# Two attention layers rewritten: heads' steps with projection units between them, one list for the weight ring, outputs turned later

## The chip, the cores and the metric

The kernel runs on one core of a Trainium2 chip. A time is device microseconds (us) of one execution; the number that counts is the median of several executions. Five engines work side by side from queues of their own: TensorE (PE: matrix products and transposes), VectorE (DVE), ScalarE (ACT), GpSimd (POOL) and SyncE (SP, which here issues nearly all transfers). They wait for each other through semaphores, and each runs its own instructions strictly in the written order.

## The reference, cut to what matters

A block of two layers (an "even" and an "odd" one) runs on 256 tokens of width 2048, and after it a second block of two layers (a linear recurrence and a differential attention), which the change does not rewrite. All numbers are float32.

```
def even_layer(x, mem, ...):
    h = rms_norm(x, norm_g) @ w_in                  # 2048 -> 832 + 3072 + 512 + 2560
    c_q, c_kv, k_pe, qkv_b, q_mem, gate = split_cols(h, EVEN_SPLITS)
    q_a = rms_norm(c_q, q_norm_g) @ w_uq            # 8 heads, 128 + 64 (the 64 rotated)
    kv_a = rms_norm(c_kv, kv_norm_g) @ w_ukv
    o_a = causal_attention(q_a, k_a, v_a)           # "MLA", 8 heads
    o_b = moba_attention(q_b, k_b, v_b)             # "MOBA", 8 heads, causal at this length
    o_m = memory_attention(q_mem, mem, ...)         # 4 heads, no mask
    y = jnp.concatenate([o_a, o_b, o_m], -1) * jax.nn.silu(gate)
    return x + y @ w_out                            # 2560 -> 2048
def odd_layer(x, mem, ...):
    h = rms_norm(x, norm_g) @ w_in                  # 2048 -> 6400
    ...    # o_c: "SWA", 16 heads of 64 in a window of 128, 2 key heads, sinks
    ...    # o_d: "DIL", 6 heads, dilated masks;  o_m: memory attention, 4 heads
    y = jnp.concatenate([o_c, o_d, o_m], -1) * jax.nn.silu(gate)
    return x + y @ w_out                            # 2304 -> 2048
# the second block needs silu(c) @ mod_w + mod_b and silu(c_ctx) @ mod_w + mod_b,
# 2048 -> 6144 in both of its layers; nothing before it does
```

## The kernel before, in words

**Products.** A product is made in chunks of 512 output columns. A *unit* is a slice of two blocks of 128 weight rows by 512 columns (512 KB). Float32 accuracy comes from three products of rounded parts: each weight is split in a high part (made by ACT, `hi`, L1004) and a low part (made by DVE, `lo`, L1419), each activation likewise, and `multiply` (L549) issues for each of the 2 token tiles and each of the 2 row blocks three matmuls, 12 in all. So a *projection unit* (P below) needs, in this order: its transfer, ACT's cast, DVE's subtraction, and then PE.

**The ring.** Weights pass through a ring of 4 slots, in three buffers (`ring` for what lands, `ring_hi`, `ring_lo`). Unit U uses slot U mod 4. SP issues the transfers in the order of the units and waits before unit U until `ring` is free of unit U-4: for a projection unit that is when its low part has been made, for a *modulation unit* (M below) when PE has used it. The cast of unit U waits until PE has multiplied unit U-4.

**Modulation units.** The second block's modulation vectors come from 24 chunks of `mod_w` with 8 units each. They need no split: `fill_mod` (L608) multiplies them as they land (8 recorded matmuls for two units). After a chunk DVE copies four partial sums out (`mod_rows`, L1487), PE adds them up (L617) and DVE stores the columns (L1496).

**Attention.** Heads are worked in pairs, a pair is a *turn*: 2 MEM, 4 MOBA, 4 MLA turns in the even layer, 4 + 4 SWA, 3 DIL and 2 MEM turns in the odd one. In `head_loop` one turn is: POOL copies q and k into a staging tile; PE transposes them (L629, L631, for MLA's rotated part L634); ACT copies them out (L1062); PE makes the scores (L645, L648); DVE scales and masks them (L1510) and takes the negated maximum (L1514); ACT takes the exponentials (L1069, L1072); PE transposes these (L657); DVE copies them (L1526); PE multiplies by the values (L673); DVE divides and gates (L1534, L1540) into a tile of its own; PE transposes the gated output (L681), and ACT and DVE split it at once into the parts of the next product (L1079, L1549). In each of the four gaps between PE's steps stand 2 modulation units, 8 in a turn, and no projection.

**The order of stages.** The even layer's input projections (14 chunks of columns, `ev_a` and `ev_b`), 6 turns, the products `uq` and `ukv` for MLA, 4 turns, the output product `ev_out`, transposes of the new x, the odd layer's input projections (`od_b`, `od_c`), 13 turns, and `od_out`. One modulation chunk is made alone within `od_c`. Scores are always 256 by 256 a head, masked or not. The results of a projection chunk leave PSUM (PE's output memory, 8 banks of 512 columns) by ACT (`evict`, L1052, with Silu for the gates); 2 of 4 banks are in use for a chunk.

## Time and profile before

| | |
|---|---|
| median of 3 executions | 2783.96 us (2781.33 to 2784.78) |
| the profiled execution | 2789.43 us |
| its span, first to last instruction | 2787.2 us |
| PE busy | 2591.3 us, 93% |
| DVE busy | 1457.0 us, 52% |
| ACT busy | 1165.8 us, 42% |
| mean granted clock of PE | 0.964 |
| transfers | 424.86 MB, 152 GB/s in the mean |

The busy times are those of the span; what is left outside of the span is 2.2 us. The granted clock is the share of full speed that PE was given: 1.00 is 2.4 GHz, 0.50 is 1.2 GHz, and a value between them is a mean over a stretch that has both. PE is the engine that is nearly always busy, so the questions to ask of the profile are where it idles, where it runs at the lower clock, and what it does in the time that is left.

### The profile page before, as it was taken

What the parts mean: (1) busy time and instruction counts of PE and PEld (TensorE: products, weight loads), DVE (VectorE), ACT (ScalarE), POOL (GpSimd) and SP (SyncE); (2) the same over time, 40 slices, a digit from 0 to 9 for tenths busy, and PEclk for the clock granted to TensorE, in tenths of its full rate; (3) what the DMA queues carried; (4) which work ended last, traced back from release to release, by engine and by line L of the source; (5) the groups of instructions that cost most, each with busy time, mean ns of one, the idle gap of its engine ahead of it and who ended that gap; (6) DMA issues with size and microseconds to landing.
All of it is one profiled execution on the core that took longest, in us unless ns stands there. A gap on an engine that the chain in (4) does not pass through costs nothing.

```text
span 2787.2 us, 33773 instructions
## 1 busy us (share of the span) xinstructions
PE 2591.3 (93%) x12110; PEld 2014.4 (72%) x12110; DVE 1457.0 (52%) x1857; ACT 1165.8 (42%) x1709; POOL 246.1 (9%) x200
## 2 busy tenths in 40 slices
PE   6999998889899997889799999999799999999988
PEld 5888885548788864448577777778677787777766
DVE  4644544444544534355546676743436565463764
ACT  5445442323444422134545555622433334243442
POOL 0000001000000000000144555300000000000000
PEclk9999999999999998699899999999999999999999
DMA  5566667675566667696323333233244334242423
GB/s 205 186 193 189 194 193 258 212 250 183 152 193 195 190 194 255 214 307 233 116 82 91 98 94 90 79 114 98 61 121 121 99 91 120 83 128 83 121 91 121
DMA packets 275085, 424.86 MB, mean 152 GB/s; under 512 B 14374, under 2 KB 92988, under 8 KB 273852
## 3 DMA queue, kind: packets, MB, share of 16 engines
q1 hardware_dynamic: 273596, 418.28, 49.1%
q10 hardware_dynamic: 1408, 5.51, 0.5%
q8 instruction: 49, 0.80, 0.1%
q14 instruction: 32, 0.26, 0.0%
HBM read 421.65 MB, written 2.10 MB: 152 GB/s over the span
## 4 chain that ended last, share of the span: by engine, by line
PE 85%; DVE 7%; ACT 4%; issue 2%; DMA 1%; SPq 0%; DVEq 0%; ACTq 0%
PE ps L549 59%; PE ps L793 13%; PE ps L608 3%; PE ps L800 2%; PE ps L673 2%; PE ps L645 1%; PE ps L617 1%; ACT ring_hi L1004 1%; DVE head_stats L1514 1%; ACT arena L1069 1%; DVE ring_lo L1419 1%; PE ps L885 1%; DVE arena L1510 1%; PE ps L903 1%; PE ps L590 1%
## 5 line engine op out<-in xcount | busy, mean ns | idle before, releaser
L1004 ACT CAST ring_hi<-ring 128x1024 fp32r<-128x1024 f32 (+2 forms) x590 | 614.7, 1044 | 1126.0 <-PE ps L549 968.0
L1419 DVE TENSOR_TENSOR ring_lo<-ring,ring_hi 128x1024 fp32r<-128x1024 f32 (+2 forms) x526 | 634.9, 1211 | 847.8 <-ACT ring_hi L1004 845.6
L549 PE MATMUL ps<-ring_hi,act_hi 128*128 128x512 f32 (+2 forms) x1272 | 496.1, 390 | 18.7 <-DVE act_lo L1458 7.6
L549 PE MATMUL ps<-ring_hi,features_hi 128*128 128x512 f32 x1152 | 463.1, 402 | 37.0 <-DVE features_lo L1771 15.3
L549 PE MATMUL ps<-ring_lo,act_hi 128*128 128x512 f32 (+2 forms) x1272 | 494.1, 388 | 0.0
L549 PE MATMUL ps<-ring_hi,act_lo 128*128 128x512 f32 (+2 forms) x1272 | 493.7, 388 | 0.0
L549 PE MATMUL ps<-ring_lo,features_hi 128*128 128x512 f32 x1152 | 453.9, 394 | 0.0
L549 PE MATMUL ps<-ring_hi,features_lo 128*128 128x512 f32 x1152 | 453.5, 394 | 0.0
L549 PEld LDWEIGHTS ps<-ring_hi,features_hi 128*128 128x128 f32 x1152 | 219.1, 190 | 106.7 <-issue 41.9
L549 PEld LDWEIGHTS ps<-ring_hi,act_hi 128*128 128x128 f32 x1272 | 242.5, 191 | 71.1 <-issue 11.6
L549 PEld LDWEIGHTS ps<-ring_lo,act_hi 128*128 128x128 f32 x1272 | 242.6, 191 | 48.4
L549 PEld LDWEIGHTS ps<-ring_hi,act_lo 128*128 128x128 f32 x1272 | 242.1, 190 | 48.2
L549 PEld LDWEIGHTS ps<-ring_hi,features_lo 128*128 128x128 f32 x1152 | 219.3, 190 | 47.3
L549 PEld LDWEIGHTS ps<-ring_lo,features_hi 128*128 128x128 f32 x1152 | 219.5, 191 | 42.9
L793 PE MATMUL ps<-features_hi,ring_hi 128*128 128x512 f32 x512 | 206.6, 403 | 3.8 <-DVEq L1777 3.8
L793 PE MATMUL ps<-features_lo,ring_hi 128*128 128x512 f32 x512 | 200.2, 391 | 0.0
L793 PE MATMUL ps<-features_hi,ring_lo 128*128 128x512 f32 x512 | 200.2, 391 | 0.0
L2049 POOL TENSOR_TENSOR ring_lo<-ring,ring_hi 128x1024 fp32r<-128x1024 f32 x64 | 168.9, 2647 | 274.9 <-ACT ring_hi L1004 274.7
L608 PE MATMUL ps<-ring,cond_t 128*32 128x512 f32 x768 | 124.6, 673 | 2.8 <-DMA ring<-in_mod_w 2.7
L2036 POOL COPY arena<-proj 128x256 f32 (+1 forms) x38 | 17.2, 452 | 1191.6 <-PE ps L631 439.8
L793 PEld LDWEIGHTS ps<-features_hi,ring_hi 128*128 128x128 f32 x512 | 96.8, 189 | 27.3 <-issue 7.6
L793 PEld LDWEIGHTS ps<-features_lo,ring_hi 128*128 128x128 f32 x512 | 96.9, 189 | 23.2 <-issue 3.6
(226 smaller groups left out, 2507.8 us busy)
## 6 DMA issues: line engine op xcount, KB each, us to landing
ring<-in_mod_w SPq DMA_DIRECT2D x192, 512.0 KB, 4.5
ring<-in_att_w_in SPq DMA_DIRECT2D x128, 512.0 KB, 3.8
ring<-in_ev_w_in SPq DMA_DIRECT2D x104, 512.0 KB, 4.3
ring<-in_od_w_in SPq DMA_DIRECT2D x96, 512.0 KB, 3.7
ring<-in_lru_w_in SPq DMA_DIRECT2D x64, 512.0 KB, 4.2
ring<-in_ev_w_out SPq DMA_DIRECT2D x40, 512.0 KB, 3.7
ring<-in_od_w_out SPq DMA_DIRECT2D x36, 512.0 KB, 4.4
ring<-in_lru_w_out SPq DMA_DIRECT2D x32, 512.0 KB, 3.7
```

The lines of the kernel that those rows point to most:

```text
L549: mm = pe.matmul(PS[:, bank, 0:n], a, w[:, k - k0, :], start=(k == 0 and j == 0), stop=(k == kt - 1 and j == 2))
L590: mm = pe.transpose(PS[:, 4 + q % 4, col:col + P], rows(tt, 2 * j + k), ident)
L608: mm = pe.matmul(PS[g:g + 32, bank, :], CS[:, 2 * k:2 * k + 32], RA[:, U % SLOTS, k % 2 * CHUNK:(k % 2 + 1) * CHUNK], start=(k < 4), stop= ...
L617: mm = pe.matmul(PS[:, bank, 2 * j:2 * j + 2], rows[:, j * P:(j + 1) * P], SEL[:], start=True, stop=True)
L645: mm = pe.matmul(PS[:, 6 + a, tt * SEQ:(tt + 1) * SEQ], qk[:, tt * P:(tt + 1) * P], qk[:, SEQ:2 * SEQ], start=True, stop=not mla)
L673: mm = pe.matmul(PS[:, 6 + a, tt * P:tt * P + w], PT[:, a, kt * SEQ + tt * P:kt * SEQ + (tt + 1) * P], v, start=(kt == 0), stop=(kt == TT ...
L793: mm = pe.matmul(PS[:, part * 2 + b, :], W[:, U % SLOTS, w], x[:, kk, :], start=(kk == 0 and j == 0), stop=(kk == KT - 1 and j == 2))
L800: mm = pe.matmul(PS[:, 4 + j, :], GW[:, b, j, :], XC[:, b, :, :].rearrange("p c s -> p (c s)"), start=True, stop=True)
L885: mm = pe.matmul(PS[:, 4 + c, :], DQK[64 * c:64 * c + 64, j, CHUNK + tt * P:CHUNK + (tt + 1) * P], DQK[64 * c:64 * c + 64, j, 0:CHUNK], st ...
L1004: act.copy(WH[:, U % SLOTS, 0:n], RA[:, U % SLOTS, 0:n]).then_inc(s_hi, 1)
L1419: dve.tensor_tensor(out=WL[:, U % SLOTS, 0:n], in0=RA[:, U % SLOTS, 0:n], in1=WH[:, U % SLOTS, 0:n].bitcast(F32), op=ALU.subtract).then_in ...
L2049: pool.tensor_tensor(out=WL[:, U % SLOTS, :], in0=RA[:, U % SLOTS, :], in1=WH[:, U % SLOTS, :].bitcast(F32), op=ALU.subtract).then_inc(s_l ...
```

## The change

Both layers are written anew around one list, `RING`, of all units in their order. The list is laid out at build time. A turn (`Turn`) now has four gaps that hold *projection units of later chunks* and modulation units together. With P for a projection unit, M for a modulation unit and a bar for each step of PE in the turn (scores, transposes of the weights of attention, values), the gaps are, as the list has them:

| turns | gaps |
|---|---|
| MEM 0, 1, MOBA 0 (even) | PPP, PPMMPPMMP, PPMMPP, PPMMP |
| MOBA 1, 3 | PPP, PPMMPPMMP, PPMMP, PPMMP |
| MOBA 2 | PPP, PPMMPMMP, PPMMP, PPMMP |
| MLA 0, 1 | MM, PMMP, MM, MM |
| MLA 2, 3 | MM, PMM, MM, MM |
| SWA, 8 turns, and DIL 0 | P, PMMPMMP, PMMP, PMM (DIL 0: third gap PMM) |
| DIL 1, 2 | P, PMMPMM, PMM, PMM |
| MEM 0, 1 (odd) | P, PMMMM, PMM, PMM; P, PMMPMM, PMM, MM |

Only the chunks that the first turns need (two of `ev_b`, three of `od_b`) are made before the turns. MLA's P are the first units of `ev_out`. The modulation chunk that stood alone is mixed into the last `od_b` chunk before the turns. Further:

- ACT and DVE follow the list: `follow` makes, for each unit of a gap, the split of the unit 4 (ACT) or 3 (DVE) places on, and evicts a chunk after its last unit.
- Three PSUM banks instead of four serve the projections of the turns, each half of a chunk is awaited and released by itself, and `multiply` now does all row blocks of one token tile before the next tile.
- Masks that leave a block empty are used: scores are 384 columns a head instead of 512, 3 blocks instead of 4 are transposed and multiplied.
- q and k are transposed straight from their rows; POOL's staging is gone. SWA's two key heads are doubled and transposed once.
- The gated output overwrites the gate; the transposes of y and their splits come later, two blocks at a time: between the `ukv` units, between the first units of `ev_out`, and beside the first 9 units of `od_out`.
- The transposes of the new x stand between the last units of `ev_out`.
- The copies of two inputs of the second block (ctx, final gain) are issued some units later in `od_out`.

```diff
-            def head_loop(h):
-                ...
-                    fill_mod(mod, 0, i)
...
+EV_PRE, OD_PRE = (6, 11), (0, 2)
+EV_FILL, OD_FILL = (0, 2, 4, 9, 1, 3, 5, 10, 7, 8), (1, 9, 3, 4, 5, 6, 10, 11, 7)
+SPREAD = ((), (0, 1), (2,), (3,))
+MLA_TURNS = lay_turns(6, [(MLA, 0, (0, 2, 0, 0)), (MLA, 1, (0, 2, 0, 0)), (MLA, 2, (0, 1, 0, 0)), (MLA, 3, (0, 1, 0, 0))],
+                      [("ev_out", u) for u in range(4, 10)], ((0,), (1,), (2,), (3,)))
...
+                for m, bank in tiles:
+                    if hold is not None and m in hold:
+                        pe.wait_ge(*hold[m])
+                    for k in range(k0, k0 + nk):
                         xh, xl = x(k, m)
...
+            def head_turn(turn):                       # PE
...
+                if h is MLA:
+                    pe.wait_ge(s_ge, evicted("ukv", i))
+                    pe.wait_ge(s_ys, n0)
+                for a in range(1 if h.pair else 2):
+                    ...                                # transposes of q and k
+                fill(turn.gaps[0])
+                if turn.mod:
+                    sum_mod(turn.mod - 1, 2 if h is MLA else MB)
+                ...                                    # scores
+                fill(turn.gaps[1])
+                ...                                    # transposes of the exponentials
+                fill(turn.gaps[2])
+                if h.mem is None:
+                    pe.wait_ge(s_ge, evicted(*value_chunk(turn)))
+                ...                                    # values
+                fill(turn.gaps[3])
...
+            def follow(units):                         # ACT
+                for unit in units:
+                    U = POS[unit]
+                    hi_to(U + SLOTS)
+                    if U in LAST_OF:
+                        evict(*LAST_OF[U])
+                    hi_to(U + SLOTS + 1)
...
+            def follow(units):                         # DVE
+                for unit in units:
+                    lo_to(POS[unit] + SLOTS)
+                    ropes_behind(*unit)
...
+            def head_turn(turn):                       # DVE
+                follow(turn.gaps[0])
+                if turn.mod:
+                    mod_columns(turn.mod - 1, 2 if h is MLA else 3)
+                ...                                    # mask, maximum
+                follow(turn.gaps[1])
+                ...                                    # copies of the transposed exponentials
+                follow(turn.gaps[2])
+                dve.wait_ge(s_ge, evicted(*gate_chunk(turn)))
+                ...                                    # division and gate
+                follow(turn.gaps[3])
+                mod_rows(turn.mod)
```

**SP's queue in a SWA turn.** Before, in the turns of the odd layer, SP issued modulation units alone. `weight_units_used` counts the units that PE has multiplied; the rows around the transfer are the loop's own.

```order
L438 DMA ring<-in_mod_w 128x2x512 [waits weight_units_used] x8
L452 UNCONDITIONAL_BRANCH
L452 ISA
L438 ISA [waits weight_units_used]
L438 DMA ring<-in_mod_w 128x2x512
L436 REGISTER_ALU
```

Now a SWA turn is this; `weights_lo_by_vector` counts the low parts made by DVE, and the name behind "waits" is what frees the slot, so it tells what stood in the slot four places earlier.

```order
L581 DMA ring<-in_od_w_in 128x2x512 [waits weights_lo_by_vector]
L581 DMA ring<-in_mod_w 128x2x512 [waits weights_lo_by_vector]
L581 DMA ring<-in_mod_w 128x2x512 [waits weight_units_used]
L581 DMA ring<-in_od_w_in 128x2x512 [waits weight_units_used]
L581 DMA ring<-in_od_w_in 128x2x512 [waits weights_lo_by_vector]
L581 DMA ring<-in_mod_w 128x2x512 [waits weight_units_used] x2
L581 DMA ring<-in_od_w_in 128x2x512 [waits weights_lo_by_vector] x2
L581 DMA ring<-in_mod_w 128x2x512 [waits weight_units_used] x2
L581 DMA ring<-in_od_w_in 128x2x512 [waits weights_lo_by_vector] x2
L581 DMA ring<-in_mod_w 128x2x512 [waits weight_units_used] x2
```

What moved: projection transfers (`in_od_w_in`) now stand between the modulation transfers, and the fourth row is a projection unit whose slot a modulation unit held.

**DVE in an MLA turn.** Before, in the MLA loop: division and gate of the turn's second head (L1534, L1540), the copy of the modulation chunk's sums (L1487), the low parts of the output (L1549), and no unit of the ring. ISA rows only set up the instruction below them.

```order
L1534 RECIPROCAL head_stats<-head_stats 128x2 [waits head_out]
L1540 ISA [waits head_recip]
L1540 SCALAR_TENSOR_TENSOR arena<-ps,head_stats,proj 128x128
L1540 ISA
L1540 SCALAR_TENSOR_TENSOR arena<-ps,head_stats,proj 128x128
L1486 ISA
L1487 COPY proj<-ps 128x512 [waits weight_units_used]
L1549 ISA [waits head_y_hi]
L1549 TENSOR_TENSOR act_lo<-ps,act_hi 128x256
L1549 ISA [waits head_y_hi]
L1549 TENSOR_TENSOR act_lo<-ps,act_hi 128x256
```

Now, at the end of the first MLA turn, from the same division to the first mask of the next turn:

```order
L1816 RECIPROCAL head_stats<-head_stats 128x2 [waits head_out]
L1822 SCALAR_TENSOR_TENSOR proj<-ps,head_stats,proj 128x128 [waits head_recip]
L1822 SCALAR_TENSOR_TENSOR proj<-ps,head_stats,proj 128x128
L1639 TENSOR_TENSOR ring_lo<-ring,ring_hi 128x1024 [waits weights_hi]
L1725 COPY proj<-ps 128x512 [waits weight_units_used]
L1733 TENSOR_TENSOR mod_t<-ps,vectors_t 128x8 [waits mod_summed]
L1786 SCALAR_TENSOR_TENSOR arena<-ps,consts_first 128x384 [waits head_scores]
```

What moved: the low part of a projection unit of the next turn (L1639) stands ahead of the copy of the modulation sums (L1725), on which the next turn's first modulation unit waits; the output's low part (L1549) is gone from here.

## Rows read from the trace of the kernel before

**Rows 1.** The page, first section: busy us, share of the span, instructions.

```profile
PE 2591.3 (93%) x12110; PEld 2014.4 (72%) x12110; DVE 1457.0 (52%) x1857; ACT 1165.8 (42%) x1709; POOL 246.1 (9%) x200
```

**Rows 2.** PE's waits: waiter <- releaser: us in total, times, longest us.

```profile
PE ps L657 <- ACT head_stats L1072: 22.9, 16, 2.2
...
PE ps L657 <- ACT arena L1069: 19.6, 26, 1.0
...
PE ps L681 <- DVE arena L1540: 12.1, 3, 4.1
```

**Rows 3.** Busy time by stage: stretch, length, busy per engine, clock, DMA, GB/s.

```profile
168.10:429.40 261.30, 261.30 (x1161) 216.25 (x1159) 119.62 (x113) 121.54 (x136) 1.43 (x4) 1.00 0.66 190
429.40:519.10 89.70, 73.46 (x505) 43.62 (x504) 49.40 (x106) 30.09 (x79) 7.70 (x20) 0.97 0.87 288
519.10:549.00 29.90, 29.84 (x120) 24.11 (x120) 12.51 (x15) 13.61 (x18) 1.65 (x4) 0.92 0.48 156
549.00:624.20 75.20, 63.83 (x384) 34.65 (x384) 32.17 (x68) 23.14 (x62) 4.95 (x12) 0.97 0.70 233
624.20:736.00 111.80, 111.77 (x482) 92.26 (x483) 52.45 (x46) 41.17 (x39) 0.00 (x0) 0.97 0.62 191
736.00:748.40 12.40, 4.09 (x32) 3.17 (x30) 10.66 (x19) 10.95 (x20) 0.00 (x0) 0.76 0.30 86
748.40:1014.70 266.30, 266.29 (x1180) 220.69 (x1184) 121.17 (x113) 117.44 (x125) 3.81 (x3) 0.99 0.61 181
1014.70:1037.00 22.30, 17.71 (x109) 10.77 (x108) 4.15 (x7) 3.94 (x7) 0.00 (x0) 0.92 0.75 245
1037.00:1256.70 219.70, 178.23 (x1052) 97.63 (x1051) 99.95 (x253) 54.16 (x163) 13.60 (x43) 0.82 0.77 257
1256.70:1357.10 100.40, 100.37 (x432) 82.58 (x432) 46.55 (x47) 46.17 (x53) 6.32 (x3) 0.98 0.68 219
sum 1189.00, PE 1106.89 PEld 825.72 DVE 548.62 ACT 462.20 POOL 39.46; mean PE 110.69 PEld 82.57 DVE 54.86 ACT 46.22 POOL 3.95
```

**Rows 4.** L549 alone in a stretch of projections: length, busy, clock.

```profile
211.60:429.40 217.80, 217.80 (x960) 1.00 0.65 188
```

**Rows 5.** A MOBA turn by time: start, length, engine, line [idle before].

```profile
459.05 1.06 PE L608 MATMUL ps<-ring,cond_t 128*32 128x512 f32 x8
...
460.04 1.99 PE L645 MATMUL ps<-arena 128*128 128x256 f32 x8
...
463.81 0.66 PE L657 MATMUL ps<-consts,arena 128*128 128x128 f32 x4 [0.61 <-ACT arena L1069]
...
466.70 2.05 PE L673 MATMUL ps<-proj,arena 128*128 x16
...
469.93 0.69 DVE L1487 COPY proj<-ps 128x512 f32<-128x512 f32 x1 [0.22 <-PE ps L608]
```

**Rows 6.** The last MOBA turn by time: uq units behind modulation units.

```profile
506.49 1.10 PE L608 MATMUL ps<-ring,cond_t 128*32 128x512 f32 x8
...
507.58 10.02 SPq L438 DMA_DIRECT2D ring<-in_ev_w_uq  x6
...
511.73 1.05 ACT L1004 CAST ring_hi<-ring 128x1024 fp32r<-128x1024 f32 x1 [5.88 <-DMA ring<-in_ev_w_uq]
...
513.38 1.05 ACT L1004 CAST ring_hi<-ring 128x1024 fp32r<-128x1024 f32 x1 [0.59 <-DMA ring<-in_ev_w_uq]
...
512.81 1.23 DVE L1419 TENSOR_TENSOR ring_lo<-ring,ring_hi 128x1024 fp32r<-128x1024 f32 x1 [5.52 <-ACT ring_hi L1004]
```

**Rows 7.** ACT by time in the second block, changing its table.

```profile
2154.07 1.28 ACT L1315 ACT_TABLE_LOAD   x1
2155.37 1.08 ACT L1315 ACTIVATE second_block<-ps 128x512 f32<-128x512 f32 x2
```

**Rows 8.** Stretches with PE idle first, columns as in rows 3.

```profile
2153.80:2157.20 3.40, 0.69 (x5) 0.54 (x4) 1.89 (x2) 3.35 (x5) 0.00 (x0) 1.00 0.54 154
2642.40:2650.60 8.20, 4.34 (x14) 3.42 (x13) 4.70 (x10) 6.50 (x13) 0.00 (x0) 0.79 0.23 77
```

More of the change, by code:

```diff
@@ new lines, with __init__, with_mod @@
+class Turn:
+    def __init__(self, number, heads, i, mod, gaps):
+        self.number, self.heads, self.i, self.mod, self.gaps = number, heads, i, mod, gaps
+        self.even = heads in (MEM_EV, MOBA, MLA)
+def with_mod(units, m, pairs):
+    out, n = [], len(units)
+    after = {}
+    for j, p in enumerate(pairs):
+        after.setdefault(-(-(j + 1) * n // (len(pairs) + 1)), []).append(p)
+    for k in range(n + 1):
+        for p in after.get(k, []):
+            out += [("mod", 8 * m + 2 * p), ("mod", 8 * m + 2 * p + 1)]
+        out += units[k:k + 1]
+    return out
@@ new lines, in lay_turns, with chunk_units @@
+def lay_turns(first, plan, units, mod_gaps):
+    turns, at = [], 0
+    for j, (heads, i, counts) in enumerate(plan):
+        number = first + j
+        m = number if number < MOD_ALONE else number + 1
+        gaps = []
+        for count, pairs in zip(counts, mod_gaps):
+            gaps.append(with_mod(units[at:at + count], m, pairs))
+            at += count
+        turns.append(Turn(number, heads, i, m, gaps))
+    assert at == len(units)
+    return turns
+def chunk_units(stage, chunks, per=8):
+    return [(stage, per * c + j) for c in chunks for j in range(per)]
@@ new lines, with _queue @@
+OD_TURNS = lay_turns(10, [(SWA[j], i, (1, 3, 2, 1)) for j in range(2) for i in range(4)]
+                     + [(DIL, 0, (1, 3, 1, 1)), (DIL, 1, (1, 2, 1, 1)), (DIL, 2, (1, 2, 1, 1)), (MEM_OD, 0, (1, 1, 1, 1)), (MEM_OD, 1, (1, 2, 1, 0))],
+                     chunk_units("od_b", OD_FILL) + chunk_units("od_c", [0]), SPREAD)
+OUT_C1_AHEAD = [("ev_out", 10 + u) for u in range(4, 10)]
+OD_LAST_PRE = with_mod(chunk_units("od_b", [8]), MOD_ALONE, range(4))
+RING = []
+def _queue(units):
+    RING.extend(units)
@@ new lines, with units_of, multiplied, unit_width @@
+CHUNK_UNITS = {"uq": 2, "ukv": 1, "ev_out": 10, "od_out": 9}
+def units_of(stage):
+    return CHUNK_UNITS.get(stage, 8)
+def multiplied(stage, c):
+    return max(POS[stage, u] for u in range(c * units_of(stage), (c + 1) * units_of(stage))) + 1
+def unit_width(stage, u):
+    if stage == "ev_a" and u >= 8:
+        return 2 * (EV_LAT - EV_CKV)
+    return 2 * (OD_IN % CHUNK) if stage == "od_c" else UNIT
+EVICTED = ([(stage, c) for stage in ("mkv0", "mkv1", "ev_a") for c in range(2)] + [("ev_b", c) for c in EV_PRE + EV_FILL]
+           + [("uq", c) for c in range(3)] + [("ukv", c) for c in range(4)] + [("od_b", c) for c in OD_PRE + (8,) + OD_FILL] + [("od_c", 0)])
@@ new lines, in rows_free, with gate_chunk, value_chunk @@
+def rows_free(bank, before):
+    return max(2 * e + w + 1 for e in range(EVICTED.index(before)) for w in range(2) if BANKS[EVICTED[e]][w] == bank)
+def gate_chunk(turn):
+    h, i = turn.heads, turn.i
+    if h is MEM_OD:
+        return ("od_b", 11) if i == 0 else ("od_c", 0)
+    if h is DIL:
+        return "od_b", 10 + i // 2
+    if h in SWA:
+        return "od_b", 8 + SWA.index(h)
+    return "ev_b", {"mem_ev": 11, "moba": 9 + i // 2, "mla": 7 + i // 2}[h.name]
+def value_chunk(turn):
+    h, i = turn.heads, turn.i
+    if h.mem is not None:
+        return None
+    if h is MLA:
+        return "ukv", i
+    return ("ev_b", 4 + i // 2) if h is MOBA else ("od_b", 6 if h is DIL else 2)
@@ new lines, in _ @@
+            pe.wait_ge(s_ge, evicted("od_c", 0))
+            for p in range(3):
+                y_transposes_of("od", p)
+            for p in range(9):
+                pe.wait_ge(s_ye, YT_AT["od", p] + 1)
+                od_out(p)
+                for q in (range(3, 5), range(5, 7), range(7, 9))[p] if p < 3 else ():
+                    if q >= 7:
+                        pe.wait_ge(s_ys, 2 * (q + 15))
+                    y_transposes_of("od", q)
+                if p == 2:
+                    sum_mod(N_MOD - 1)
@@ L771, in _ @@
+            for u in range(9, 36):
+                od_out(u)
             pe.wait_ge(s_re, RES0["lru_out"])
```

1117 lines of the change are left out of this document (600 added, 517 removed).

## The prediction

> **What bounds the kernel now.** First the page: PE is busy for 2591.3 us, 93% of the span [rows 1]; no other engine passes 52%. So a change pays where PE idles or runs slowly, or where it takes work from PE. Second the waits of PE: in the turns PE waits before the transposes of the exponentials (L657) for ACT, 22.9 and 19.6 us in all, and before the transposes of y (L681) for DVE, 12.1 us in three waits of about 4 us, one at the end of each run of turns [rows 2]. Third the stretches, cut by stage, from the first `ev_b` unit at 168.1 us to the last `od_out` unit at 1357.1 us [rows 3]. They are 1189.0 us long and PE is busy for 1106.9, so 82.1 us are idle: 16.2 in the first six turns (89.70 less 73.46), 11.4 in the MLA turns, 41.5 in the 13 odd ones, 8.3 at the transposes of x. The projections between them have none. The same rows hold a second loss, the clock: 1.00 in the projections, 0.82 in the odd turns. Busy time times the missing share is, in the order of the rows, 0, 2.2, 2.4, 1.9, 3.4, 1.0, 2.7, 1.4, 32.1 and 2.0, together 49 us. So PE has 1106.9 - 49 = 1058 us of work at full clock in 1189 us.
>
> **What the change takes from PE.** Matmuls of projections and modulation stay as many as they were. In the 19 masked turns half of the score records shrink to half (8 records in 1.92 us, from 460.04 to the next step: -0.5), 2 of 8 transposes go (4 take 0.66: -0.3) and 4 of 16 value records (2.05 us: -0.5) [rows 5]; that is 1.3 a turn, 25 us. MLA's rotated part and SWA's doubled keys add some 4. So 29 us, and 1029 us of work are left. If PE never waited, the stretch would end 1189 - 1029 = 160 us earlier. POOL's copies go too, but PE waited little for them; the matmul order within a unit costs nothing (the same 12 matmuls), in the second block it moves a wait by a few matmuls, which I put at 0, with 2 us to either side.
>
> **The filling.** A projection unit (P) takes 12 records of 217.8/960 us, 2.72 us [rows 4]; two modulation units (M) take 0.99 us, from 459.05 to 460.04, so 0.5 each [rows 5]. The chain from scores to exponentials is about 5 us; a gap of PPMMPPMMP lasts 15.6 us and even PMMPMMP 10.2 us. So the waits of L657 go, all 42.5 us, and the clock has dense work.
>
> **What is late next: the ring.** An M leaves its slot only when PE has used it, and the unit four places on may then be a P, which needs transfer, cast and subtraction. The trace shows this once, where `uq` follows the last turn. PE ends a pair of M begun at 506.49; the transfers are issued from 507.58; the casts are at 511.73 and 513.38, 1.05 us each; the first subtraction runs from 512.81 for 1.23 us [rows 6]. So a P in the slot of the pair's first M is ready at 514.04, 6.5 us after PE left the pair, and one in the slot of the second at 513.38 + 1.05 + 1.23 = 515.66, 8.1 us after. In PMMPMMP the last P stands in the slot of the second M (the row of SP's queue that waits for `weight_units_used` ahead of `in_od_w_in`). Between them PE has one P and two M, 3.7 us: it waits 4.4. The bounds are 2.8 (ready as a first one) and 4.4; I take 3.9, nearer to the row that shows it. Such places: 8 SWA turns, DIL 0, MOBA 2, and the chunk ahead of the odd turns, 11 of them, 43 us. In PPMMPPMMP two P and more stand between, 6.6 us or more against 6.5: nothing. Elsewhere:
> - DIL 1, 2: two such P each with 4.4 and 5.7 us of cover, 5 us a turn, 10 us. Odd MEM turns: PMMMM covers only 3.4 us of the exponentials' chain, and `od_c` units are half as long; 8 us a turn, 16 us. First `od_out` unit: silu eviction, division, then transposes, ACT and DVE for the first pair of y: 5 us.
> - MLA: the low part of the next turn's P stands on DVE ahead of the copy of the modulation sums, and PE's first M of the next turn waits for that copy. The P is in the slot of the last pair's first M, so the copy ends 6.5 + 0.7 us later [rows 5, 6]; PE has 0.5 (M) + 1 (waiting for the division) + 1.3 (transposes), so it waits 4.4 at three turn starts, 13. Waits of 1.5 inside each turn and 3.5 at the exit to `ev_out` make it 23 us (10 to 30).
> - Start of the first turn, MOBA's small waits, the way into MLA: 10 us.
> - ACT changes tables between Silu and Exp. Eight silu chunks now leave within turns. A change is 1.28 us, and the activation follows at once [rows 7]. The next chunk's second tile needs the bank after 1.36 us of matmuls; table and first half (1.28 + 0.54) end at 1.8, so 0.5 each, 4 us.
>
> What the Trainium skill says of the last point, in ScalarE: Activation LUTs, section "What ACT_TABLE_LOAD costs", is more: about 1.28 us of load and as much again of drain at each change, 2.66 us, with the advice to group by table set, which this change goes against. The trace shows the load and no drain behind it. By the page's figure the term would be some 15 us instead of 4.
>
> - The clock: after an idle time of 2.7 us PE stays at 1.00, after one of 3.9 us the next stretch shows 0.79, a piece at 1.2 GHz [rows 8]. Some 15 new waits lie between; 1 us each, 15 us.
>
> **The sum.** 43 + 10 + 16 + 5 + 23 + 10 + 4 + 15 = 126 us of new waits against 160: the change wins 34 us. The profiled execution would be 2789.4 - 34 = 2755 us (span 2753); the median of the runs shown lies 5.5 us lower, 2784.0 - 34 = 2750 us. Tell apart from no change can a measurement 0.2%, 5.6 us. With every wait at its low bound (11 x 2.8, MLA 10, the others halved, the clock 0) it is some 65 us, a gain of 95; with the high ones (48, 30, 45, 10, and 25 for the clock) 160, a gain of nothing.
>
> **Rivals.**
> *The cover holds* (2688 us). Transfers may be issued earlier than I place them and land in 3.5 us, DVE and ACT may be ahead, and the clock never falls. For it: in the projections DVE is busy for 46% and ACT for 47% (119.62 and 121.54 of 261.3) [rows 3], so nothing but latency stands against it. Against it: [rows 6]. Waits of 65 us: 2784 - 95.
> *The clock falls with each wait* (2809 us, slower). A wait of 4 us once a turn, then a stretch at 1.2 GHz, in which P takes 5.4 us. For it: the odd turns had waits of at most 2.2 us and yet 0.82 [rows 2, 3]. Against: they were full of short, narrow steps, and now two thirds of a turn are dense matmuls. Price: these turns now hold 72 P, 11 us of `od_c` and 13 times 10 us of M and steps, 337 us; at 0.82 they take 411, 74 more. 160 - 111 (126 without the clock term) - 74 = -25. It decides from 0.9 downwards.
>
> The Trainium skill speaks for this one, in TensorE: Matmul & The Clock Gate, section "HAM oscillation — how this bites in real kernels": where a wait for a transfer comes back in every tile, the clock is lost anew each time. The trace agrees in kind (0.79 after 3.9 us), not in 2.7 us.
>
> *The transfers are the bound* (2784 us, no change). 478 units pass the ring in the stretch. Two back to back landed 1.65 us apart by their casts (511.73 and 513.38) [rows 6]: 789 us, less than 1029. Only the turns with few P come near. Little speaks for it.
>
> **Chances.** Forecast 0.50, cover holds 0.25, clock 0.15, transfers or anything else that gives the gain back 0.10. The time is the forecast's, 2750 us, its own range 2722 to 2778. The range for 8 in 10 goes from 2692, short of the second case, to 2792, short of the third. Faster by more than 0.2%: all of the first two and half of the last, 0.80; the other half is no change, 0.05; slower 0.15.
>
> **What would show it.** Right: waits of L657 for ACT gone; per SWA turn one wait of PE's projections of 3 to 4 us for DVE's low part, beside a shorter one for a modulation transfer, and nothing of the kind in MEM and MOBA turns except MOBA 2; at three MLA turn starts PE waiting for the copy of the sums; the stretch up to the end of `od_out` 20 to 50 us shorter, and from there to the end the same length. The filling is wrong if L657 still waits for ACT. The sum is wrong if the clock of the odd stage stays under 0.9, or if the SWA turns have no wait at all.

## The result, and the profile after

The changed kernel takes 2827.51 us (median of 4, 2824.62 to 2831.30), the one before, beside it, 2784.37. The ratio is 1.0151, 95% interval 1.0126 to 1.0177: 42 us slower, where 34 us faster was forecast. The profiled execution took 2831.3 us, its span is 2829.2.

First the page of the changed kernel, its first section (busy us, share of the span, instructions). PE is busy for 9 us more than in [rows 1], although it has 126 matmuls fewer.

```profile
PE 2600.0 (92%) x11984; PEld 2005.9 (71%) x11984; DVE 1435.1 (51%) x1900; ACT 1158.1 (41%) x1698; POOL 215.4 (8%) x120
```

Next the waits of PE in the changed kernel (us in total, times, longest), to be read against [rows 2].

```profile
PE ps L674 <- DVE ring_lo L1639: 77.0, 43, 4.6
PE ps L743 <- DVE proj L1725: 19.2, 3, 7.0
...
PE ps L674 <- DVE act_lo L1772: 7.3, 1, 7.3
PE ps L743 <- DMA ring<-in_mod_w: 6.0, 10, 1.3
```

The waits for the exponentials, 42.5 us, are gone. In their place stand waits for low parts of projection units (77.0 us), the copy of the modulation sums at three MLA turn starts (19.2), the low part of y ahead of `od_out` (7.3), and modulation transfers (6.0).

Then the stretch from the first `ev_b` unit to the last `od_out` unit, cut by stage, columns as in [rows 3]: `ev_b` ahead of the turns, even turns with their projections, `ukv`, MLA turns, `ev_out`, `od_b` ahead of the turns, the chunk with the lone modulation chunk, odd turns with their projections, `od_out`, and last what follows it.

```profile
168.10:213.90 45.80, 44.50 (x202) 36.35 (x201) 24.26 (x34) 25.75 (x39) 0.00 (x0) 1.00 0.64 195
213.90:554.35 340.45, 313.92 (x1487) 235.65 (x1487) 142.11 (x192) 130.59 (x179) 0.00 (x0) 0.96 0.62 205
554.35:568.90 14.55, 14.15 (x66) 11.64 (x66) 10.30 (x18) 9.51 (x16) 0.00 (x0) 0.88 0.38 115
568.90:687.80 118.90, 93.14 (x416) 53.97 (x416) 28.72 (x66) 23.23 (x58) 0.00 (x0) 0.76 0.50 167
687.80:779.70 91.90, 91.88 (x420) 76.12 (x421) 52.55 (x61) 39.30 (x48) 0.00 (x0) 0.98 0.58 187
779.70:837.90 58.20, 58.20 (x263) 48.04 (x261) 28.84 (x32) 29.55 (x35) 0.00 (x0) 1.00 0.59 176
837.90:867.00 29.10, 23.61 (x109) 15.37 (x109) 11.37 (x23) 8.72 (x9) 2.27 (x6) 0.94 0.74 253
867.00:1289.00 422.00, 371.05 (x1889) 252.34 (x1887) 171.17 (x340) 135.24 (x247) 0.00 (x0) 0.94 0.66 220
1289.00:1401.80 112.80, 105.52 (x478) 87.39 (x476) 57.65 (x67) 54.59 (x66) 6.14 (x3) 0.95 0.66 218
1401.80:2829.20 1427.40, 1339.93 (x5985) 1066.71 (x5984) 816.96 (x926) 612.86 (x881) 206.75 (x108) 0.97 0.33 98
```

The last row is what lies behind the rewritten layers: 1427.4 us, as before (2787.2 - 1357.1 = 1430.1). So all of the loss in the profiled execution is in the stretch, which is now 1233.7 us long instead of 1189.0. Length less busy time, row by row, is 117.7 us of idle time. Busy time times the missing share of the clock is 0, 12.6, 1.7, 22.4, 1.8, 0, 1.4, 22.3 and 5.3, together 67.5. The account of the stretch, beside what was forecast:

| us | before | forecast | after |
|---|---|---|---|
| work at full clock | 1058 | 1029 | 1048 |
| PE idle | 82 | 111 | 118 |
| lost to the clock | 49 | 15 | 68 |
| the stretch | 1189 | 1155 | 1234 |

The work at full clock is what is left of a length without the other two; with granted clocks of two digits it is good to a few us. The idle time was forecast within 7 us. The clock is off by 53, the work by 19.

Where the clock goes is seen in one SWA turn. First PE, ACT, DVE and SP by time (start, us, engine, line, [idle before]), without the rows of weight loads and the projection matmuls ahead; then three stretches around the wait.

```profile
950.38 1.14 PE L743 MATMUL ps<-ring,cond_t 128*32 128x512 f32 x8
...
951.48 0.88 SPq L581 DMA_DIRECT2D ring<-in_mod_w  x2
951.75 1.04 ACT L1222 CAST ring_hi<-ring 128x1024 fp32r<-128x1024 f32 x1 [2.43 <-DMA ring<-in_od_w_in]
952.83 2.52 DVE L1639 TENSOR_TENSOR ring_lo<-ring,ring_hi 128x1024 fp32r<-128x1024 f32 x2 [6.06 <-ACT ring_hi L1222]
...
954.11 0.50 PE L674 MATMUL ps<-ring_hi,act_hi 128*128 128x512 f32 x1 [2.59 <-DVE ring_lo L1639]
```

```profile
926.00:951.00 25.00, 23.65 (x130) 15.77 (x128) 11.06 (x25) 9.07 (x18) 0.00 (x0) 1.00 0.63 212
954.10:957.50 3.40, 3.39 (x9) 2.72 (x10) 1.23 (x1) 0.00 (x0) 0.00 (x0) 0.58 1.02 372
957.60:971.00 13.40, 13.40 (x74) 9.47 (x72) 4.89 (x12) 3.14 (x3) 0.00 (x0) 0.98 0.55 194
```

PE waits 2.59 us for the low part of the last unit of the gap PMMPMMP, the place where a wait was forecast. Then it works for 3.4 us at a granted clock of 0.58, mostly at 1.2 GHz, and at 0.98 after that. The wait of 2.6 us costs 1.4 us more (3.39 x 0.42).

The start of the second MLA turn shows the order on two engines at once (weight loads, transfers and ACT's other copies are left out):

```profile
589.35 0.38 PE L804 MATMUL ps<-consts,proj 128*64 128x128 f32 x2
...
593.79 1.04 ACT L1222 CAST ring_hi<-ring 128x1024 fp32r<-128x1024 f32 x1 [12.39 <-DMA ring<-in_ev_w_out]
594.74 0.58 ACT L1317 COPY arena<-ps 128x512 f32<-128x512 f32 x1
594.87 1.22 DVE L1639 TENSOR_TENSOR ring_lo<-ring,ring_hi 128x1024 fp32r<-128x1024 f32 x1 [6.78 <-ACT ring_hi L1222]
...
596.01 0.68 DVE L1725 COPY proj<-ps 128x512 f32<-128x512 f32 x1
...
596.75 1.94 PE L743 MATMUL ps<-ring,cond_t 128*32 128x512 f32 x8 [7.01 <-DVE proj L1725]
...
598.61 1.87 PE L754 MATMUL ps<-row_sums,proj 128*128 128x2 f32 x8
```

The copy of the sums (L1725) stands behind the low part (L1639), that behind ACT's cast (L1222), and that waits for a transfer. ACT's copies of q and k (L1317) stand behind the same cast. PE idles for 7.01 us, and its next steps run at half speed: the granted clock from 596.7 to 600.3 is 0.50, and eight small matmuls (L754) take 1.87 us, where 1.05 us is their time at full clock (at 448.07 in the run `plain` below).

### The profile page after: what moved, and what is told of

Same layout as the page of the kernel before. It is cut to its first block, busy times and chain, and to the rows that moved or that the text cites. A ratio compares the mean times of both kernels' runs of the same rounds, so it can differ in the third digit from the quotient of the medians.

```text
span 2829.2 us, 31394 instructions
## 1 busy us (share of the span) xinstructions
PE 2600.0 (92%) x11984; PEld 2005.9 (71%) x11984; DVE 1435.1 (51%) x1900; ACT 1158.1 (41%) x1698; POOL 215.4 (8%) x120
## 4 chain that ended last, share of the span: by engine, by line
PE 79%; DMA 9%; DVE 6%; ACT 5%; issue 1%; SPq 1%; ACTq 0%; DVEq 0%
PE ps L674 55%; PE ps L1011 12%; DMA ring<-in_od_w_in 5%; DVE ring_lo L1639 2%; ACT ring_hi L1222 2%; DMA ring<-in_ev_w_in 2%; PE ps L743 2%; PE ps L1018 2%; PE ps L822 1%; PE ps L1103 1%; DMA ring<-in_ev_w_out 1%; PE ps L754 1%; PE ps L1121 1%; PE ps L719 1%; PE ps L844 1%
## 5 line engine op out<-in xcount | busy, mean ns | idle before, releaser
L1222 ACT CAST ring_hi<-ring 128x1024 fp32r<-128x1024 f32 (+2 forms) x590 | 611.6, 1038 | 1337.4 <-PE ps L674 776.8
L1639 DVE TENSOR_TENSOR ring_lo<-ring,ring_hi 128x1024 fp32r<-128x1024 f32 (+2 forms) x526 | 634.2, 1209 | 898.2 <-ACT ring_hi L1222 893.4
L674 PE MATMUL ps<-ring_hi,act_hi 128*128 128x512 f32 (+2 forms) x1272 | 528.8, 416 | 92.6 <-DVE ring_lo L1639 73.7
L674 PE MATMUL ps<-ring_lo,act_hi 128*128 128x512 f32 (+2 forms) x1272 | 508.1, 399 | 0.0
L674 PE MATMUL ps<-ring_hi,act_lo 128*128 128x512 f32 (+2 forms) x1272 | 507.5, 399 | 0.0
L674 PEld LDWEIGHTS ps<-ring_hi,act_hi 128*128 128x128 f32 x1272 | 250.0, 197 | 203.6 <-DVE ring_lo L1639 113.2
L674 PEld LDWEIGHTS ps<-ring_hi,act_lo 128*128 128x128 f32 x1272 | 250.1, 197 | 54.1
L674 PEld LDWEIGHTS ps<-ring_lo,act_hi 128*128 128x128 f32 x1272 | 251.1, 197 | 46.1
L743 PE MATMUL ps<-ring,cond_t 128*32 128x512 f32 x768 | 123.9, 624 | 25.3 <-DVE proj L1725 19.2
L1011 PEld LDWEIGHTS ps<-features_hi,ring_lo 128*128 128x128 f32 x512 | 96.7, 189 | 20.3
```

Of the source, the lines that this page charges most:

```text
L674: mm = pe.matmul(PS[:, bank, 0:n], a, w[:, k - k0, :], start=(k == k_first and j == 0), stop=(k == k_last and j == 2))
L743: mm = pe.matmul(PS[g:g + 32, MB, :], CS[:, 2 * k:2 * k + 32], RA[:, U % SLOTS, k % 2 * CHUNK:(k % 2 + 1) * CHUNK], start=(k < 4), stop=(k ...
L1011: mm = pe.matmul(PS[:, part * 2 + b, :], W[:, U % SLOTS, w], x[:, kk, :], start=(kk == 0 and j == 0), stop=(kk == KT - 1 and j == 2))
L1222: act.copy(WH[:, U % SLOTS, 0:n], RA[:, U % SLOTS, 0:n]).then_inc(s_hi, 1)
L1639: dve.tensor_tensor(out=WL[:, U % SLOTS, 0:n], in0=RA[:, U % SLOTS, 0:n], in1=WH[:, U % SLOTS, 0:n].bitcast(F32), op=ALU.subtract).then_in ...
```

## The experiments

Times are given as the ratio to the kernel before, timed on the same chip. The changed kernel has 1.0151; 0.01 is 28 us. The runs stand on three chips, so what is won or lost is told by the ratios and not by the medians.

**Matmuls in the waits (`warm`).** `dense(n, bank)` issues n matmuls of 512 columns (384 where a first column is given) of `act_hi` by itself into a bank that is free there.

```diff
+                    if wait and at == len(units) - 1 and stage != "mod" and units[at - 1][0] == "mod":
+                        dense(wait, 4)          # wait = 10, second gap, not MLA
...
+                if h is MLA and i:
+                    dense(34, 2, P)             # ahead of the first gap; 20 more at MLA's exit
```

> The changed kernel, with matmuls that nobody reads put where PE waits: ten of 512 columns (2.3 us) ahead of the last projection unit of the second gap in the 15 turns where that unit follows modulation units (it waited 2.5 to 3.0 us), 34 of 384 columns (5.8 us) at the starts of MLA turns 1 to 3 (5.7 to 7.0 us waited), 20 of them at MLA's exit (4.6 us). Nothing is made earlier, so the waits only turn into work. Theory 'the clock': these waits cost the granted clock as well, some 55 us at the lower level behind the waits of the even and odd turns and 60 us in the MLA turns. Then the clock of the MLA turns goes from 0.76 to 0.95 or more, of the odd turns from 0.94 to 0.97, and the time falls by 40 to 55 us, to 2772 to 2787. Rival 'idle time only' (the clock falls for the narrow modulation matmuls or the short attention steps, waits or not): clock and time unchanged, or up to 10 us longer.

Measured: 1.0015 (0.9993 to 1.0036), so 38 us won, though the added matmuls make nothing that is used. Even, MLA and odd turns in this run:

```profile
214.10:542.50 328.40, 318.55 (x1552) 239.57 (x1553) 144.46 (x194) 132.27 (x180) 0.00 (x0) 1.00 0.64 215
554.50:681.30 126.80, 120.06 (x582) 81.76 (x583) 36.43 (x77) 27.43 (x62) 0.00 (x0) 0.85 0.52 175
846.50:1258.00 411.50, 381.10 (x1982) 258.55 (x1980) 172.96 (x341) 137.78 (x249) 0.00 (x0) 0.98 0.67 229
```

The clock is 1.00 instead of 0.96, 0.85 instead of 0.76, and 0.98 instead of 0.94. In MLA it rises less than the 0.95 that were expected; what is left there was not looked for. That idle time costs the clock is shown.

**Narrow matmuls in the waits (`warm_narrow`).**

```diff
-                    pe.matmul(PS[:, bank, first:CHUNK], ATH[:, 0:P], ATH[:, first:CHUNK], start=True, stop=True)
+                    pe.matmul(PS[0:32, bank, first:CHUNK], ATH[:, 0:32], ATH[:, first:CHUNK], start=True, stop=True)
```

> The run with dense matmuls in the waits, but the added matmuls use 32 columns of the array instead of 128 (as the modulation matmuls do), as many and as long ones, at the same places. Theory 'any work keeps the clock': as with the dense ones, 2791, clock of the MLA turns as there. Rival 'the columns of the array count': narrow matmuls keep the clock no better than idling, the stretches at the lower clock come back, 2815 to 2827.

Measured: 0.9988 (0.9966 to 1.0010), at least as fast as with the wide ones. The even, MLA and odd turns show 1.00, 0.90 and 0.98. Matmuls of 32 columns keep the clock no worse than those of 128, so that the modulation units are narrow is not what lowers it. It is the idle time.

**The order on DVE (`rows_first`), and on ACT as well (`rows_act`).**

```diff
+                if h is MLA:                    # DVE
+                    mod_rows(turn.mod)
                 follow(turn.gaps[3])
...
+                if h is MLA and turn.i:         # ACT, behind the copies of q and k; rows_act only
+                    follow(MLA_TURNS[turn.i - 1].gaps[3])
```

> The changed kernel, with the copy of the modulation sums ahead of the low parts on DVE at the end of the four MLA turns. PE's wait for that copy (19.2 us in three) goes. Theory 'two engines': ACT has the same order (the cast of the next projection unit stands ahead of the copies of q and k), so PE waits before the scores instead, and of 7.0 us only some 4.4 are won at each start: 13 us of waiting, and with the clock 15 to 20 us, 2807 to 2812. Rival 'DVE alone': all 19 us and the clock behind them, 35 us, 2792. Rival 'the unit itself': the projection unit behind the scores is late by what was won, nothing is won.

> As the run before this one, and on ACT the cast of the next turn's projection unit stands behind the copies of q and k. Theory 'two engines': now the whole wait goes at the three starts, 19 us, and most of the 57 us at the lower clock in the MLA turns, 20 us more: 2827 - 39 = 2788. Rival 'the unit itself' (its transfer lands 8 us after the slot is free, its cast and low part follow): a wait of 2 to 4 us before the first projection unit takes the place, and the win is 20 us or less, 2807 or above.

Measured: 1.0088 (1.0057 to 1.0119) and 1.0009 (0.9983 to 1.0034): 18 and 40 us won. The MLA turns with the first `ev_out` units, 130.0 us long and at 0.76 in the changed kernel, in the two runs:

```profile
560.60:674.00 113.40, 99.29 (x460) 59.39 (x461) 36.56 (x77) 27.33 (x62) 0.00 (x0) 0.85 0.59 199
```

```profile
562.90:664.20 101.30, 90.91 (x460) 54.84 (x461) 36.52 (x77) 27.70 (x62) 0.00 (x0) 0.93 0.68 223
```

In `rows_first` PE's wait for the copy of the sums (19.2 us) is gone, and in its place stand 3.6 us before the scores for ACT's copies (L822 for L1319), as the theory 'two engines' has it in kind; it had put some 8 us there. In `rows_act` these are gone too. The wait is the queues' order, not the unit's transfer. With DVE's order mended ACT's still holds PE; ACT's alone was not tried. The stretch tells 29 of the 40 us, the rest is not placed.

**Half of each modulation transfer (`half_mod`).** SP moves 256 of the 512 columns, so the modulation vectors are made from other numbers.

```diff
-                    unit(U, t["mod_w_2"][layer], 2 * j, 2, chunk * CHUNK, CHUNK)
+                    unit(U, t["mod_w_2"][layer], 2 * j, 2, chunk * CHUNK, CHUNK, part=2)
```

> The changed kernel, but a modulation unit moves only the first half of its columns (256 KB instead of 512 KB); PE multiplies as before, with what stands in the other half of the slot. The modulation sums are so computed from other numbers. Theory 'burst': behind a modulation pair SP issues up to four transfers at once, they land 1.3 us apart, and the projection unit among the last is late by the two modulation transfers ahead of it. With those at half, it lands 1.3 us earlier: PE's wait for low parts falls from 77 us to about 45, with the clock 35 to 45 us are won, 2785 to 2792. Rival 'latency': the 4 us from issue to landing and the 2.3 us of cast and subtraction are all there is, the waits stay within 10 us of 77 and the time within 10 us of 2827.

Measured: 1.0021 (0.9998 to 1.0043), 36 us won, but not as expected:

```profile
PE ps L674 <- DVE ring_lo L1639: 71.1, 42, 4.8
```

The waits for low parts fell by 6 us, not by 32. The odd turns became 20 us shorter (402.2 instead of 422.4), of which idle time is 6 (402.20 - 357.12 = 45.1 against 50.9); 9 are busy time of the modulation matmuls (58.8 instead of 67.6 us for 416 records; the last section tells why a late transfer lengthens them), the rest other busy time, which holds the clock. The time fits the theory, its place does not. That the transfers' bytes count is shown. That they count as a burst ahead of the projection unit is not: the wait it was to shorten stayed.

**The order of units in the SWA turns (`regroup`, `alt`).** The units of each of the 8 turns are laid out anew, where they were P|PMMPMMP|PMMP|PMM.

```diff
+for _turn in OD_TURNS[:8]:
+    singles(_turn, "P|PMMPPMM|PMM|PPMM")          # regroup
+    singles(_turn, "P|MPMPMPM|PMPM|PMM")          # alt
```

> The changed kernel with the units of the 8 SWA turns in the order P|PMMPPMM|PMM|PPMM: modulation units in pairs as before, two projection units between the pairs where they can be. Theory 'the slot': waits of 2.6 us a turn instead of 3.9, in two pieces of about 1 to 1.5 us, behind which the clock stays: 10 us of waiting and 8 us of clock: 2827 - 18 = 2809. Rival 'rate': 2827.

> The changed kernel with the units of the 8 SWA turns in the order P|MPMPMPM|PMPM|PMM instead of P|PMMPMMP|PMMP|PMM (the same units in the same gaps, but modulation units single). Theory 'the slot' (a projection unit is late where it follows a modulation unit into its slot with less than 6.5 us of PE's work between): of four such places a turn two are left with more cover, the waits of a turn fall from 3.9 us to 2.4 and none is over 1 us, so the clock stays: 12 us of waiting and 10 us of clock in the eight turns, less 5 us for 24 more changes between the two kinds of matmul: 2827 - 17 = 2810. Rival 'rate' (the transfers of a turn take as long in any order): the waits stay 31 us in eight turns and the changes of kind are added: 2832.

Measured: 1.0078 (1.0044 to 1.0113), 20 us won, and 1.0214 (1.0185 to 1.0243), 18 us lost. Regrouped, the odd turns are 405.7 us long instead of 422.4. With single units PE's waits are as the slot theory has them, 42.7 us for low parts down to 17.4 in the odd turns, but two new costs stand beside them. The groups of that run in the odd turns:

```profile
L685 PE MATMUL ps<-ring_hi,act_hi 128*128 128x512 f32 (+1 forms) x320 | 135.7, 424 | 17.7 <-DVE ring_lo L1650 17.4
...
L754 PE MATMUL ps<-ring,cond_t 128*32 128x512 f32 x416 | 91.8, 632 | 1.8 <-DMA ring<-in_mod_w 1.6
...
L765 PE MATMUL ps<-row_sums,arena 128*128 128x2 f32 x104 | 15.5, 271 | 21.1 <-DVE arena L1736 21.1
```

The same groups of the changed kernel:

```profile
L674 PE MATMUL ps<-ring_hi,act_hi 128*128 128x512 f32 (+1 forms) x320 | 139.3, 435 | 43.2 <-DVE ring_lo L1639 42.7 <-ACT proj L1295 0.3
...
L743 PE MATMUL ps<-ring,cond_t 128*32 128x512 f32 x416 | 67.6, 613 | 2.6 <-DMA ring<-in_mod_w 2.5
...
L754 PE MATMUL ps<-row_sums,arena 128*128 128x2 f32 x104 | 12.6, 243 | 3.6 <-DVE arena L1725 3.6
```

The same 416 modulation matmuls take 24 us more, while those of the projections take 388 instead of 398 us. And PE waits 21.1 instead of 3.6 us for the copy of the sums, which now stands behind a late low part on DVE, as in MLA.

**The last odd turn (`od_exit`).** On DVE the division, the copy of the sums and the first y stand ahead of `od_out`'s low parts. On ACT the first y stands ahead of their casts.

```diff
+                if last:                        # DVE, ahead of follow(turn.gaps[2])
+                    mod_rows(turn.mod)
+                    y_lo_of("od", 0)
...
+                    y_hi_of("od", 0)            # ACT, behind the last eviction
```

> The changed kernel, but in the last odd turn DVE does the division ahead of the low parts of od_out's first units, and ACT and DVE split the first pair of y ahead of the casts and low parts behind it. PE waited 7.3 us for that low part (1290.6 to 1297.8) and ran 10 us at the lower clock behind it. Theory 'queue order': od_out's first unit is then ready by its own transfer (landed 1290.6 plus 2.3 us), 4.8 us earlier, and with the clock 5 to 8 us are won: 2820. Rival 'the transfer': the next units are late by the same, nothing is won, 2827.

Measured: 1.0147 (1.0118 to 1.0176), no difference to 1.0151 that can be told. The stage itself, from the last turn's end, became 5.7 us shorter, 108.6 instead of 114.3 with a clock of 0.98 instead of 0.96:

```profile
1291.40:1400.00 108.60, 104.92 (x478) 86.86 (x476) 58.02 (x63) 55.77 (x67) 7.29 (x4) 0.98 0.68 230
```

Only the profile speaks for the queue's order here.

**No mixing (`plain`).** The projections stand ahead of the turns (`uq` and MLA's `ev_out` units behind them), the modulation pairs in the turns as before; the rest of the change stays, but for the PSUM bank of the modulation sums.

```diff
-SPREAD = ((), (0, 1), (2,), (3,))
+SPREAD = ((0,), (1,), (2,), (3,))
...
+            fill(EV_AHEAD)
             for turn in EV_TURNS:
...
+            fill(OD_AHEAD)
             for turn in OD_TURNS:
```

> The change without its mixing: all projections of a layer ahead of its turns (uq between the even turns and ukv, ev_out behind MLA), two modulation units in each of a turn's four gaps as in the kernel before; the halved masked blocks, the missing staging, the late transposes of y and the order within a unit stay as in the changed kernel. Theory 'mixing costs': the projections run at their 2.72 us again, the even turns with their projections take 314 us instead of 342, MLA with its 91 instead of 119, the odd ones 402 instead of 422, although the waits for the exponentials and the clock of 0.82 in the odd turns come back: 2827 - 76 = 2752. Rival 'the waits for the exponentials cost as much': within 10 us of 2827. Rival 'something else in the change costs' (its copies, the late transposes): 2800 or above.

Measured: 0.9830 (0.9805 to 0.9855), median 2747.15 us: by the ratios 89 us faster than the changed kernel and 47 faster than the one before. The profiled execution took 2757.5, 10 us above the median. The even turns with seven `uq` units behind them, the MLA turns with the first `ev_out` units, and all projections and turns of the odd layer behind its third chunk:

```profile
433.00:536.30 103.30, 90.58 (x533) 52.83 (x534) 46.34 (x101) 33.91 (x77) 0.00 (x0) 0.98 0.85 287
547.20:644.90 97.70, 92.05 (x461) 54.31 (x460) 37.49 (x77) 27.98 (x62) 0.00 (x0) 0.91 0.67 232
815.80:1214.70 398.90, 365.76 (x1891) 248.42 (x1889) 173.83 (x338) 127.34 (x239) 0.00 (x0) 0.95 0.73 231
```

The odd part is 23.5 us shorter than mixed, the MLA part 32.3, although PE again waits for exponentials, 33.0 us in all. The longer part of these, and all its waits for low parts in the whole kernel:

```profile
PE ps L833 <- ACT head_stats L1335: 17.4, 16, 1.8
PE ps L678 <- DVE ring_lo L1650: 17.3, 8, 3.7
```

**Matmuls in the waits for exponentials: in the kernel before (`before_dense`), and without mixing (`plain_dense`).** The edit of the first is shown; the second has the same in its SWA turns and three such matmuls in each other turn but MLA's.

```diff
+                        for _ in range((8, 4)[a] if pair else 0):
+                            pe.matmul(PS[:, 2, :], ATH[:, 18 * SEQ:18 * SEQ + P], ATH[:, 18 * SEQ:20 * SEQ], start=True, stop=True)
                         pe.wait_ge(s_ex, n(a, 1))
```

> The kernel before, with matmuls that nobody reads ahead of the waits for the exponentials in the 8 SWA turns: 8 of 512 columns (1.8 us) ahead of the first head's transposes (2.0 to 2.2 us waited), 4 (0.9 us) ahead of the second's (1.2 us waited). Theory 'the clock falls with PE's density': the odd turns run at 0.82 because their steps are short, so dense work in the gaps lifts the clock there to 0.9 or more; 10 to 15 us of the 32 us lost are won: 2770 to 2775. Rival 'the kind of matmul' (modulation matmuls of 32 columns and the narrow steps count as little, whatever stands between): clock 0.82 to 0.84, time as before or up to 5 us longer.

> The same, with matmuls that nobody reads in the waits for the exponentials: 8 and 4 of 512 columns in a SWA turn, 3 in the other turns but MLA's. By what such matmuls won in the kernel before (22 us): 2730. If the turns without staging have shorter waits, so that the added matmuls outlast them: as without them, 2752, or up to 10 us more.

Measured: 0.9921 (0.9894 to 0.9949) and 0.9842 (0.9810 to 0.9873). In the kernel before, 22 us are won, more than expected; its odd turns are 193.2 us long, not 219.7 as in [rows 3], at a clock of 0.98 instead of 0.82:

```profile
1036.00:1229.20 193.20, 173.21 (x1141) 99.84 (x1141) 99.41 (x252) 54.03 (x163) 13.52 (x43) 0.98 0.86 289
```

Without mixing nothing is won in the median, where 22 us were expected: the clock of the odd part rises from 0.95 to 1.00, but PE's busy time from 365.8 to 377.9 us.

```profile
810.70:1203.60 392.90, 377.90 (x2003) 262.88 (x2001) 175.02 (x340) 128.34 (x240) 0.00 (x0) 1.00 0.74 236
```

**What won, together (`best`).** `rows_act`, `regroup` and `od_exit`, with 9 matmuls in the wait of the second gap and 18 at MLA's exit.

```diff
-                fill(turn.gaps[1])
+                fill(turn.gaps[1], 0 if h is MLA else 9)
```

> The changed kernel with what won put together: the two orders on DVE and ACT in the MLA turns (39 us by their run), the SWA turns regrouped (18 us), the last odd turn's order (0 to 6 us), and nine dense matmuls in the wait of the second gap of the even turns and the first DIL turn (10 us or more by the stretch of the even turns in the run with dense matmuls). If the parts add up, 2827 - 39 - 18 - 3 - 12 = 2755; if each only moves a wait that another one hides, 2785 or above.

Measured: 0.9844 (0.9810 to 0.9879), median 2752.94 us on a chip where the kernel before takes 2793.97. By the ratios 86 us are won over the changed kernel, where 72 were expected; the two intervals leave some 12 us to either side. So no part is hidden by another. With `plain` at 0.9830 (0.9805 to 0.9855) the two cannot be told apart: mending the order, with matmuls in what waits are left, wins as much as taking the mixing out.

## Why the prediction was wrong

**Right.** The bound is PE, and the change acts in the stretch alone. The waits of L657 went. The ring's wait came where it was placed: 2.6 us per SWA turn for the low part, with shorter ones for modulation transfers; I took 3.9 us a turn, and 2.8 as the lowest. MLA came out at 25.8 us of idle time (118.90 - 93.14) against 23: three starts of 7.0, 6.5 and 5.7 instead of 4.4, an exit of 4.6, less within the turns. `rows_act` confirms the mechanism, which the forecast had seen on DVE but not on ACT. Idle time in all was 118 us against 111. PE's waits for evictions are 8.6 and 1.6 us in the whole kernel against 3.1 before, where I put 4 for the table changes; but in the longest one (3.15 us, at 499.4) no table is loaded, ACT's eviction stands behind a cast that waited for its transfer.

**Right in the sum only.** For PPMMPPMMP I forecast no wait, since two projection units cover it. It waits 2.5 to 3.0 us in each of five turns, as here in the second even turn:

```profile
291.89 1.40 SPq L581 DMA_DIRECT2D ring<-in_mod_w  x2
293.34 5.59 SPq L581 DMA_DIRECT2D ring<-in_ev_w_in  x3
...
300.30 1.04 ACT L1222 CAST ring_hi<-ring 128x1024 fp32r<-128x1024 f32 x1 [8.30 <-DMA ring<-in_ev_w_in]
...
302.66 0.78 PE L674 MATMUL ps<-ring_hi,act_hi 128*128 128x512 f32 x1 [2.56 <-DVE ring_lo L1639]
```

I counted from the slot's release to one transfer's landing. The unit was issued at 293.34, right behind a pair of modulation units, and its cast began 7 us later. These 13 us made good what the SWA turns did not cost (8 x 1.3 = 10 us), so that the idle time comes out within 7 us is in part luck.

**Wrong: the clock's term, 15 us, measured 68.** The step that failed is "after an idle time of 2.7 us PE stays at 1.00, after one of 3.9 us the next stretch shows 0.79 [rows 8]; some 15 new waits lie between; 1 us each". I took a bound between two cases from a part of the kernel in which PE had worked densely, and I let the 49 us that the old stretch lost vanish with it. After 2.6 us PE did fall, in seven of the eight SWA turns: the lower level is granted within 1 us of the wait's end or before it. The number of waits was off as well: 26 in the stretch are 2 us or longer, and 68 us over 26 waits are 2.6 us each, not 1. In MLA, waits of 6 to 7 us were followed by steps at half speed, 22 us by the row. `warm`, with 38 us won by matmuls that only fill the waits, shows that this is the waits' doing for most of the 53 us. The rival "the clock falls with each wait" was the right one in kind and sign. It was priced at 0.82 for all of a turn, and came out at 0.94 to 0.96 in the large stages and 0.76 in MLA. Its sum of 2809 us lies on the right side and 18 us short, and it had a chance of 0.15.

The sentence that the Trainium skill put beside that rival (TensorE: Matmul & The Clock Gate, section "HAM oscillation — how this bites in real kernels": a wait that recurs in every tile loses the clock anew) agrees with the trace and with `warm`: the clock fell anew in seven of eight SWA turns.

**Wrong: the work, 1029 us, measured 1048.** Between projections a modulation pair costs more than the 1.0 us at which it was taken:

```profile
961.74 0.39 PE L674 MATMUL ps<-ring_hi,act_lo 128*128 128x512 f32 x1
962.06 1.07 PE L743 MATMUL ps<-ring,cond_t 128*32 128x512 f32 x8
963.06 0.50 PE L674 MATMUL ps<-ring_hi,act_hi 128*128 128x512 f32 x1
963.39 0.39 PE L674 MATMUL ps<-ring_lo,act_hi 128*128 128x512 f32 x1
```

From the last projection matmul to the next lie 1.32 us, of which 0.23 are that matmul's own, and the first behind the pair takes 0.33 instead of 0.23. So a pair costs 1.09 + 0.10 = 1.19, 0.2 more than in [rows 5]; over some 80 pairs beside projections that would be 16 us. This is an estimate, and it does not show where the 19 us are, since in [rows 5] the attention steps beside a pair pay for the change as well.

A count over both traces does more. It takes each matmul from its start to the next one's start or its own end, times the granted clock:

| us at full clock, in the stretch | before | after | `plain` |
|---|---|---|---|
| projections | 767 | 795 | 770 |
| modulation | 106 | 116 | 128 |
| all other steps | 184 | 138 | 157 |

So the smaller attention steps gave back 46 us, more than the 29 that I took, and the count cannot part what the cut blocks gave from what such steps no longer pay beside modulation. The step that failed is "Matmuls of projections and modulation stay as many as they were", read as if they cost the same: they cost 38 us more, and 38 less the 17 that the steps gave beyond the forecast is, within the rounding, what the work was off. In the count a projection matmul takes 225 ns between its like, 309 ahead of a modulation pair and 322 to 337 as the first behind one or behind an attention step. `plain` has the projections back at 770. And nine pairs are torn by a late second transfer, four before; each half takes as long as a pair (last section).

**So** 34 us of gain became a loss of 42: 53 by the clock, 19 by the work, 7 by idle time, less 3 that the part behind the stretch was shorter. `plain` tells what the mixing itself was worth. It took away waits for exponentials of 33 us (42 in the kernel before) and put others there that cost more, and lower clock with them; what else the change does wins 47 us.

What stays open: why most waits of 2.6 us are followed by the lower clock and a few are not (in the SWA turn with the wait that ends at 1061.5 and in DIL 0 it stays at 1.00), and how much of `half_mod`'s gain is the burst.

## What to carry to other kernels

Work put into an engine's waits wins only if its own inputs are ready. Ask of each moved unit what its transfer, cast and slot wait for, and what stands behind it in the queues of the engines that prepare it. Price a recurring wait of PE at its length and the clock behind it (here 68 us beside 118 us of idle time), and test that price by filling the wait with matmuls that nobody reads; where this wins, the waits are the place to look.

## What was not expected of the hardware

- Fillers of 32 columns keep the clock as well as those of 128 (0.9988 against 1.0015, intervals that overlap).
- A single modulation unit takes PE as long as a pair. Four records by themselves, in `alt`:

```profile
911.08 1.05 PE L754 MATMUL ps<-ring,cond_t 128*32 128x512 f32 x4
```

The pair above has 1.07 us for eight. One unit fills two of the array's four groups of 32 columns and a pair all four, so by these two durations the groups work side by side. `alt` splits three pairs in each of 8 turns: 24 times 1 us is its 24 us.
- A late transfer does the same. Where the second unit of a pair lands late, PE starts the first alone. In `plain` this happens to 19 of the 96 pairs, and the 768 modulation records are busy for 145.4 us, 123.9 in the changed kernel. By 1 us each some 19 us are left to win there, an estimate.
- In the kernel before, 12 added matmuls in each of 8 turns made the whole 22 us faster.
